# Branch products and sums moved to PSUM, and a first weight chunk with both tiles side by side

## The chip, the cores and the metric

The kernel runs on one core of one Trainium2 chip. The metric is the device time of one execution in microseconds (us). Five engines work side by side: TensorE (PE in the profile, its weight loads PEld), VectorE (DVE), ScalarE (ACT), GpSimd (POOL) and SyncE (SP, which issues transfers). On-chip memory is SBUF, and PSUM with eight banks of 128 x 512 float32; here four banks are called gemm0 to gemm3, four aux0 to aux3.

## The reference

Two transformer blocks on 256 tokens of width 1024, in float32. What is computed around the change, shortened:

```python
# first block
h = rmsnorm(x, norm1_g); z = h @ w_in            # first section of w_in: conv_in0..3
ya = conformer_conv(a_val, a_gate, ...)          # ... @ w_conv_out
yb = attention(...) @ w_fox_out
mix = (sigmoid(g_a) * ya + sigmoid(g_b) * yb) @ w_out       # kernel: mix_out
x = x + mix                                      # then expert layer, 64 chunks u and 64 ev
# second block
proj   = einsum("bsnc,ncd->bsnd", [out_a, out_b, out_c], w_branch)
merged = sum_n sigmoid(z_gate)[n] * proj[n]      # three gated branches
x = x + merged @ w_out                           # kernel: out2
# then the feed-forward layer and the final norm
```

## The kernel before, in words

Activations lie transposed, channels on partitions, as eight planes k of 128 x 256. Every weight matrix is cut into tiles of 128 x 1024, which give 128 output channels for all 256 tokens; two tiles (v = 0 and 1) make a chunk, whose two outputs fill one gemm bank. To keep float32 accuracy each factor is split into a rounded part ("hi") and the rest ("lo"), and a tile is 24 matmuls: eight hi x hi, eight with the activation's rest, eight with the weight's rest. The stages around a tile: SP loads `raw` (two buffers per v), ACT rounds it into `w_hi[v]` (L1285, in `round_tile`), POOL subtracts to get `w_lo[v]` (L460, in `subtract`), PE multiplies (L670 and L675 in `product_tile`; L691, L697, L716 and L722 in `paced_product`, which is used where the activation arrives in parts). There is one `w_hi` and one `w_lo` per v, so the rounding of the next tile v waits for `hi_used[v]`, and POOL's subtraction for the tile before it to be done. The order on each engine is the order of the code: ACT's `look_ahead` puts the weight roundings between its other work.

Three places matter.

- **The start.** PE runs 13 warming matmuls (L748), then the first chunk: tile 0 in `first_tile` (L734, L737, L742), tile 1 in `product_tile`. It works on x times gain, not yet normalised. ACT rounds x in four pairs of planes (L1323), rounds tile 1 and then squares x (L1328); DVE makes the rests (L1911) and adds the squares pair by pair (L1917, L1921, L1923); PE sums over partitions with a matrix of ones (L788); ACT takes the root (L1230), DVE the reciprocal (L1862) and the normalised planes (L1874), ACT rounds these (L1240), DVE forms h_lo (L1870). Chunk 1 (order[1]) still uses the unnormalised x; chunk 2 is the first with h, in `paced_product`.
- **fox_out to mix_out.** For each of the four chunks of fox_out, DVE multiplies the gate plane by the bank (L2076), adds the other branch (L2078), ACT rounds the sum (L1457), and DVE forms the rest (L2071, in `mix_rest`). mix_out opens with `paced_product`, whose parts wait for `y_rounded` and `y_split`.
- **branch2 and branch1 to out2.** `merge(b, i)` multiplies gate and bank (L2452) and adds to `merged` (L2456) for b = 2 and then b = 1; after b = 1 ACT rounds (L1750) and DVE forms the rest (L2461). Between the two lies the third gate's product, gate1. out2 opens with `paced_product` too. branch tiles are 128 x 768, 18 matmuls each.

`ga`, `gb`, `gate`, `merged` and `sq` are parts of one SBUF tensor, `big`, by which name they stand in the profile. Lines of the adds:

```python
dve.tensor_tensor(a, a, b, ALU.add).then_inc(mix_ready, 1)                     # L2078
dve.tensor_tensor(y_lo[:, part, :], ga[:, part, :], y_hi[:, part, :], ALU.subtract)   # L2071
```

Of the kernel before, what the change touches and what calls it, by code (L numbers as in the profile page):

```python
# [34 lines left out]
ALU = mybir.AluOpType  # L35
ACT = mybir.ActivationFunctionType
# [130 lines left out]
def build(nc, t):  # L167
    plan, order = plan_chunks()
    ctx = ExitStack()
    with ctx:  # L170
# [326 lines left out]
        def _(sp):  # L497
# [47 lines left out]
            sp.dma_start(params[:, GAIN1], t["params"][:, GAIN1]).then_inc(params_in, 16)  # L545
            load(order[0], 0, t["w_conv_in0"][0])
            for n in range(4):
                part = slice(2 * n, 2 * n + 2)
                sp.dma_start(xres[:, part, :], t["xT"].rearrange("(k p) t -> p k t", p=P)[:, part, :]).then_inc(x_in[n], 16)
            load(order[0], 1, t["w_conv_in0"][1])  # L550
            sp.dma_start(params[:, GAIN1.stop:], t["params"][:, GAIN1.stop:]).then_inc(params_in, 16)

            for name, chunks in plan.items():
# [3 lines left out]
                for i, c in enumerate(chunks):  # L557
                    for n, v in enumerate(c.landing):
                        if c.index == 0:
                            continue  # L560
                        if name in PACKED:
                            load_packed(name, c, v, 2 * i + v)
                        else:
                            load(c, v, t[f"w_{name}"][len(c.landing) * i + n])
                if name == "mem_k":
# [80 lines left out]
        def _(pe):  # L646
# [11 lines left out]
            def product_tile(c, v, m, it=None, x=(h_hi, h_lo), steps=KD, rest=None):  # L658
# [7 lines left out]
                for n, act_part in enumerate(x):  # L666
                    for k in range(steps):
# [58 lines left out]
            def first_tile(c, x, x_rest):  # L726

                out = pair(gemm[c.bank])[:, 0, :]
                hi, lo = by_k(w_hi[0], P), by_k(w_lo[0], P)
                pe.wait_ge(hi_ready[0], 1)  # L730
                for k in range(KD):
                    if k % 2 == 0:
                        pe.wait_ge(h_rounded, k // 2 + 1)
                    pe.matmul(out, hi[:, k, :], x[:, k, :], start=(k == 0), stop=False)  # L734
                    if k == 0:
                        pe.wait_ge(lo_ready[0], 1)
                    mm = pe.matmul(out, lo[:, k, :], x[:, k, :], start=False, stop=False)  # L737
                mm.then_inc(tile_done[0], 1)
                for k in range(KD):
                    if k % 2 == 0:  # L740
                        pe.wait_ge(h_split, k // 2 + 1)
                    mm = pe.matmul(out, hi[:, k, :], x_rest[:, k, :], start=False, stop=(k == KD - 1))  # L742
                mm.then_inc(hi_used[0], 1)

# [471 lines left out]
        def _(act):  # L1216
# [102 lines left out]
            act.wait_ge(params_in, 16)  # L1319
            for n in range(4):  # L1320
                act.wait_ge(x_in[n], 16)
# [3 lines left out]
            look_ahead(0)  # L1325
# [16 lines left out]
            act.wait_ge(params_in, 32)  # L1342
# [110 lines left out]
            for i in range(4):  # L1453
# [3 lines left out]
                act.activation(y_hi[:, part, :], ga[:, part, :], ACT.Copy).then_inc(y_rounded, 1)  # L1457
# [288 lines left out]
            for i in range(4):  # L1746
# [3 lines left out]
                act.activation(x_hi[:, part, :], merged[:, part, :], ACT.Copy).then_inc(m_rounded, 1)  # L1750
# [60 lines left out]
        def _(dve):  # L1811
# [95 lines left out]
            dve.wait_ge(params_in, 16)  # L1907
# [6 lines left out]
            subtract(dve, order[0], tiles=(1,))  # L1914
            running = aux[0][:, 0:T]
            dve.wait_ge(squared, 1)
            dve.tensor_tensor(running, sq[:, 0, :], sq[:, 1, :], ALU.add).then_inc(paired, 1)  # L1917
            for n in range(1, 4):
                dve.wait_ge(squared, n + 1)
                dve.wait_ge(paired, n)  # L1920
                step(dve.tensor_tensor(running, sq[:, 2 * n, :], running, ALU.add))  # L1921
                settle()
                dve.tensor_tensor(sq[:, 0, :] if n == 3 else running, sq[:, 2 * n + 1, :], running,  # L1923
# [22 lines left out]
            dve.wait_ge(params_in, 32)  # L1946
# [121 lines left out]
            def mix_rest(i):  # L2068
                part = slice(2 * i, 2 * i + 2)
                dve.wait_ge(y_rounded, 2 + i + 1)  # L2070
                dve.tensor_tensor(y_lo[:, part, :], ga[:, part, :], y_hi[:, part, :], ALU.subtract).then_inc(y_split, 1)  # L2071
# [372 lines left out]
            def merge(b, i):  # L2444
# [7 lines left out]
                dve.tensor_tensor(g, g, pair(gemm[c.bank]), ALU.mult).then_inc(evacuated[c.bank], 1)  # L2452
# [216 lines left out]
```

## Time and profile before

| | |
|---|---|
| median of 3 runs (lowest, highest) | 1609.11 us (1608.95, 1610.35) |
| profiled execution, its span | 1608.7 us, 1607.0 us |
| PE busy | 1587.3 us, 99% |
| DVE, POOL, ACT busy | 1101.3, 894.6, 882.2 us |
| DMA | 277.01 MB, mean 172 GB/s |

Busy times overlap, and a pipelined matmul is counted as busy from its start to its modelled end, so 99% does not mean that the matrix unit never waits; its waits are read from gaps between starts. Idle time of the other engines costs nothing unless PE waits for them.

### The profile page before, as it was taken

To read this page: it belongs to the slowest core of one execution; us is meant where nothing else is said; L and a number is where in the kernel's file an instruction comes from. 1 tells how busy PE (TensorE), PEld (TensorE's weight loads), DVE (VectorE), ACT (ScalarE), POOL (GpSimd) and SP (SyncE) were. 2 spreads that over 40 slices of the span, in tenths; PEclk is the share of its full clock that TensorE was granted. 3 is DMA by queue.
4 is the path that set the end of the run, shared out by engine and by line. 5 is a ranking of instruction groups with operands and counts; after the bars stand their busy time and mean duration, and the time that the engine had idled before them with its cause. 6 is when DMAs were issued, how large, how long until landed. Compare 5 with 4: busy or idle time off the path is not lost.

```text
span 1607.0 us, 33462 instructions
## 1 busy us (share of the span) xinstructions
PE 1587.3 (99%) x12561; PEld 1494.1 (93%) x12561; DVE 1101.3 (69%) x1869; ACT 882.2 (55%) x1241; POOL 894.6 (56%) x413
## 2 busy tenths in 40 slices
PE   9999999999999999999999999999999999999998
PEld 7999899999999999998888888889998999999998
DVE  7998645779943777778888666676847396555522
ACT  6567765454454444444444445457667654676652
POOL 7787468868885000000000244458876589788886
PEclk9999999999999999999999999999999999999999
DMA  6565345556566555555655666655543465566663
GB/s 216 166 194 156 105 132 178 189 174 191 184 183 189 165 180 170 171 158 183 179 162 183 211 191 195 192 183 165 179 138 111 115 179 173 175 194 185 191 186 119
DMA packets 86232, 277.01 MB, mean 172 GB/s; under 512 B 11248, under 2 KB 18176, under 8 KB 86144
## 3 DMA queue, kind: packets, MB, share of 16 engines
q1 hardware_dynamic: 85872, 274.77, 55.7%
q8 instruction: 58, 0.95, 0.3%
q0 software_dynamic: 272, 1.05, 0.2%
q14 instruction: 30, 0.25, 0.1%
HBM read 274.73 MB, written 1.05 MB: 172 GB/s over the span
## 4 chain that ended last, share of the span: by engine, by line
PE 92%; DVE 3%; issue 2%; POOL 2%; ACT 1%; DMA 0%; ACTq 0%; DVEq 0%; SPq 0%; POOLq 0%
PE gemm L670 36%; PE gemm L941 22%; PE gemm L675 19%; PE aux L1192 4%; PE gemm L771 3%; PE aux L921 2%; POOL w_lo L460 1%; PE gemm L716 1%; PE gemm L1192 1%; PE gemm L691 1%; PE aux L1047 0%; PE aux L891 0%; PE gemm L757 0%; DVE h_lo L1870 0%; ACT w_hi L1285 0%
## 5 line engine op out<-in xcount | busy, mean ns | idle before, releaser
L460 POOL TENSOR_TENSOR w_lo<-raw,w_hi 128x1024 fp32r<-128x1024 f32 (+1 forms) x330 | 797.6, 2426 | 298.3 <-ACT w_hi L1285 290.2
L1285 ACT ACTIVATE w_hi<-raw 128x1024 fp32r<-128x1024 f32 (+1 forms) x492 | 516.1, 1051 | 581.6 <-PE gemm L670 322.3
L670 PE MATMUL gemm<-h_lo,w_hi 128*128 128x256 f32 x2144 | 294.2, 279 | 0.9 <-issue 0.9
L670 PE MATMUL gemm<-h_hi,w_hi 128*128 128x256 f32 x2096 | 293.3, 282 | 0.4 <-ACT w_hi L1285 0.3
L675 PE MATMUL gemm<-h_hi,w_lo 128*128 128x256 f32 x2096 | 288.9, 280 | 1.4 <-POOL w_lo L460 0.9
L670 PEld LDWEIGHTS gemm<-h_lo,w_hi 128*128 128x128 f32 x2144 | 269.1, 188 | 1.4 <-issue 1.3
L460 DVE TENSOR_TENSOR w_lo<-raw,w_hi 128x1024 fp32r<-128x1024 f32 x162 | 196.7, 1223 | 105.2 <-ACT w_hi L1285 104.6
L670 PEld LDWEIGHTS gemm<-h_hi,w_hi 128*128 128x128 f32 x2096 | 264.2, 188 | 3.3 <-issue 1.6
L675 PEld LDWEIGHTS gemm<-h_hi,w_lo 128*128 128x128 f32 x2096 | 263.0, 188 | 3.9 <-POOL w_lo L460 2.8
L941 PE MATMUL gemm<-w_hi,act_parts 128*128 128x512 f32 x1024 | 254.9, 391 | 0.4 <-ACT act_parts L1486 0.4
L941 PEld LDWEIGHTS gemm<-w_hi,act_parts 128*128 128x128 f32 x1024 | 191.0, 188 | 39.6 <-issue 0.5
L616 POOL DMA_DIRECT2D small<-in_memT x1 | 1.0, 1029 | 383.6 <-DVE big L2216 383.6
L941 PE MATMUL gemm<-w_lo,act_parts 128*128 128x512 f32 x512 | 136.9, 389 | 0.0
L2222 DVE TENSOR_TENSOR act_parts<-big,act_parts 128x512 fp32r<-128x512 f32 x64 | 89.4, 1396 | 48.3 <-ACT act_parts L1486 48.3
L941 PEld LDWEIGHTS gemm<-w_lo,act_parts 128*128 128x128 f32 x512 | 96.0, 188 | 20.2 <-DVE w_lo L460 0.3
L1959 DVE SCALAR_TENSOR_TENSOR aux<-big,params,aux 128x256 f32<-128x256 f32 x240 | 94.7, 504 | 0.0
L456 POOL TENSOR_TENSOR w_lo<-raw,w_hi 128x768 fp32r<-128x768 f32 x30 | 61.0, 2035 | 17.6 <-ACT w_hi L1282 16.6
L2208 DVE TENSOR_TENSOR small<-small 128x512 f16<-128x512 f16 x128 | 57.2, 489 | 0.0
L2515 DVE SCALAR_TENSOR_TENSOR big<-gemm,params,big 128x255 f32<-128x255 f32 (+1 forms) x96 | 39.7, 476 | 25.0 <-ACT big L1763 25.0
L2205 DVE TENSOR_TENSOR small<-small 128x1024 f16<-128x1024 f16 x64 | 46.1, 720 | 0.0
L2216 DVE SCALAR_TENSOR_TENSOR big<-aux,big 128x512 f32 x64 | 41.1, 686 | 0.0
L1486 ACT ACTIVATE act_parts<-big 128x512 fp32r (+1 forms) x64 | 40.0, 627 | 0.2 <-issue 0.2
(425 smaller groups left out, 2085.1 us busy)
## 6 DMA issues: line engine op xcount, KB each, us to landing
raw<-in_w_u SPq DMA_DIRECT2D x128, 512.0 KB, 3.6
raw<-in_w_ev SPq DMA_DIRECT2D x128, 512.0 KB, 3.9
raw<-in_w_up SPq DMA_DIRECT2D x48, 512.0 KB, 4.3
raw<-in_w_gate SPq DMA_DIRECT2D x24, 512.0 KB, 3.6
raw<-in_w_down SPq DMA_DIRECT2D x24, 512.0 KB, 4.3
raw<-in_w_conv_in SPq DMA_DIRECT2D x16, 512.0 KB, 4.3
raw<-in_w_peer_q SPq DMA_DIRECT2D x16, 512.0 KB, 3.5
raw<-in_w_branch SPq DMA_DIRECT2D x24, 288.0 KB, 2.9
```

The source lines that it names most:

```text
L456: eng.tensor_tensor(lo[:, :, 0:C96], by_k(raw[c.raw][v], C96), hi[:, :, 0:C96], ALU.subtract)
L460: eng.tensor_tensor(w_lo[v][:, 0:n], raw[c.raw][v][:, 0:n], w_hi[v][:, 0:n], ALU.subtract).then_inc(lo_ready[v], 1)
L670: mm = pe.matmul(out, w[:, k, :], act_part[:, k, :], start=(n == k == 0), stop=False)
L675: mm = pe.matmul(out, w[:, k, :], x[0][:, k, :], start=False, stop=(k == steps - 1))
L771: mm = pe.matmul(pair(gemm[c.bank])[:, tt, :], x[:, v * KD // 2 + k, tt * P:(tt + 1) * P], w[:, k, :], start=(begins and tt == k == 0), st ...
L941: mm = pe.matmul(gemm[2 * half + tt][:, :], a[:, c.raw, v, tt * P:(tt + 1) * P], w[v][:, half * (D // 2):(half + 1) * (D // 2)], start=(op ...
L1192: mm = pe.matmul(out, w[v][:, k * P:(k + 1) * P], x[:, g * KD + k, :], start=(g == k == 0 and (v == 0 or pr == 3) and w is w_hi and x is f ...
L1285: act.activation(w_hi[v][:, 0:n], raw[c.raw][v][:, 0:n], ACT.Copy).then_inc(hi_ready[v], 1)
L1959: ins = dve.scalar_tensor_tensor(acc, zc[:, k, w:w + T], tap, acc, ALU.mult, ALU.add)
L2205: dve.tensor_tensor(hot2[:, b], each(iota2, P), along(e2T[:, tokens], P), ALU.is_equal)
L2208: ins = dve.tensor_tensor(hot1[:, b, part], hot[:, b], along(gate_parts[:, part, tokens], P // 2), ALU.mult)
L2222: dve.tensor_tensor(a_lo[:, c.raw, :, :], act_peer[:, plane, :], a_hi[:, c.raw, :, :], ALU.subtract).then_inc(a_split, 1)
```

## The change

(1) The gated products of fox_out, branch2 and branch1 go to an aux bank in PSUM, and so do the sums of fox_out and branch1; ACT rounds from there and DVE takes the rest from there. The sum of branch2 still goes to SBUF. (2) The first chunk interleaves its two tiles by pairs of planes as x arrives; SP loads tile 0, the first part of x, tile 1, then the other three parts; the first gains come by ACT's queue; the other parameters come behind chunk 1. ACT rounds tile 1 after the first pair of x, and DVE subtracts it after its first pair. (3) The squares are added in three steps of 128 x 512 in place of seven of 128 x 256, and the sum over partitions becomes two matmuls, placed inside chunk 1's first tile.

```diff
-            sp.dma_start(params[:, GAIN1], t["params"][:, GAIN1]).then_inc(params_in, 16)
-            load(order[0], 0, t["w_conv_in0"][0])
-            for n in range(4):
+            def load_x(n):
                 part = slice(2 * n, 2 * n + 2)
                 sp.dma_start(xres[:, part, :], ...).then_inc(x_in[n], 16)
+            load(order[0], 0, t["w_conv_in0"][0])
+            load_x(0)
             load(order[0], 1, t["w_conv_in0"][1])
-            sp.dma_start(params[:, GAIN1.stop:], t["params"][:, GAIN1.stop:]).then_inc(params_in, 16)
+            for n in range(1, 4):
+                load_x(n)
...
+                    if c.index == 1:
+                        sp.dma_start(params[:, GAIN1.stop:], ...).then_inc(params_in, 16)
...
+            def first_chunk(c, xh, xl):
...
+                for g in (1, 2):
+                    pe.wait_ge(h_rounded, g + 1)
+                    part(hi, 0, xh, g)
+                    part(lo, 0, xh, g)
+                    part(hi, 1, xh, g)
...
+                for g in (2, 3):
+                    pe.wait_ge(h_split, g + 1)
+                    mm = part(hi, 0, xl, g, ends=True)
                 mm.then_inc(hi_used[0], 1)
+                for g in (1, 2, 3):
+                    mm = part(hi, 1, xl, g)
+                mm.then_inc(hi_used[1], 1)
+                for g in (1, 2, 3):
+                    mm = part(lo, 1, xh, g, ends=True)
+                mm.then_inc(tile_done[1], 1)
+
+            def sum_first():
+                pe.wait_ge(paired, 4)
+                for k in range(2):
+                    mm = pe.matmul(aux[3][:, 0:T], ones[:, :], sq[:, k, :], start=(k == 0), stop=(k == 1))
+                mm.then_inc(sumsq, 1)
...
-            first_tile(order[0], *start_parts)
-            product_tile(order[0], 1, P, x=start_parts)
-            sum_gathered(0)
-            product(order[1], P, x=start_parts)
+            first_chunk(order[0], *start_parts)
+            product_tile(order[1], 0, P, x=start_parts, between=sum_first)
+            product_tile(order[1], 1, P, x=start_parts)
...
+            act.dma_start(params[:, GAIN1], t["params"][:, GAIN1]).then_inc(x_in[0], 16)
...
-                act.activation(y_hi[:, part, :], ga[:, part, :], ACT.Copy).then_inc(y_rounded, 1)
+                act.activation(y_hi[:, part, :], pair(aux[i]), ACT.Copy).then_inc(y_rounded, 1)
...
-                act.activation(x_hi[:, part, :], merged[:, part, :], ACT.Copy).then_inc(m_rounded, 1)
+                act.activation(x_hi[:, part, :], pair(aux[i]), ACT.Copy).then_inc(m_rounded, 1)
...
+            running = pair(aux[0])
+            dve.wait_ge(squared, 2)
+            dve.tensor_tensor(running, sq[:, 0:2, :], sq[:, 2:4, :], ALU.add).then_inc(paired, 2)
...
-                dve.tensor_tensor(b, b, pair(gemm[c.bank]), ALU.mult).then_inc(evacuated[c.bank], 1)
+                dve.tensor_tensor(pair(aux[i]), b, pair(gemm[c.bank]), ALU.mult).then_inc(evacuated[c.bank], 1)
                 moved(dve, [c, plan["conv_out"][i]])
-                dve.tensor_tensor(a, a, b, ALU.add).then_inc(mix_ready, 1)
+                dve.tensor_tensor(pair(aux[i]), a, pair(aux[i]), ALU.add).then_inc(mix_ready, 1)
...
-                dve.tensor_tensor(g, g, pair(gemm[c.bank]), ALU.mult).then_inc(evacuated[c.bank], 1)
+                gated = pair(aux[i])
+                dve.tensor_tensor(gated, g, pair(gemm[c.bank]), ALU.mult).then_inc(evacuated[c.bank], 1)
...
-                dve.tensor_tensor(m, m, g, ALU.add).then_inc(merge_done, 1)
+                dve.tensor_tensor(gated if b == 1 else m, m, gated, ALU.add).then_inc(merge_done, 1)
...
-                dve.tensor_tensor(m_lo[:, part, :], merged[:, part, :], x_hi[:, part, :], ALU.subtract).then_inc(m_split, 1)
+                dve.tensor_tensor(m_lo[:, part, :], pair(aux[i]), x_hi[:, part, :], ALU.subtract).then_inc(m_split, 1)
```

PE's order at the start, before, from the first tile to the sum over partitions (gemm0 is the first chunk's bank; w_hi0 and w_hi1 are its tiles 0 and 1; x_hi and x_lo are x times gain, rounded and rest):

```order
L737 MATMUL gemm0<-x_hi,w_lo0 128x256
L742 MATMUL gemm0<-x_lo,w_hi0 128x256 x8
L670 MATMUL gemm0<-x_hi,w_hi1 128x256 x8
L670 MATMUL gemm0<-x_lo,w_hi1 128x256 x8
L675 MATMUL gemm0<-x_hi,w_lo1 128x256 x8
L788 MATMUL aux3<-big,ones 128x256
L670 MATMUL gemm1<-x_hi,w_hi0 128x256 x8
```

PE's order there now, from the third pair of planes on:

```order
L740 MATMUL gemm0<-x_hi,w_lo1 128x256 x2
L740 MATMUL gemm0<-x_lo,w_hi0 128x256 x2
L740 MATMUL gemm0<-x_hi,w_hi0 128x256 x2
L740 MATMUL gemm0<-x_hi,w_lo0 128x256 x2
L740 MATMUL gemm0<-x_hi,w_hi1 128x256 x2
L740 MATMUL gemm0<-x_lo,w_hi0 128x256 x4
L740 MATMUL gemm0<-x_lo,w_hi1 128x256 x6
L740 MATMUL gemm0<-x_hi,w_lo1 128x256 x6
L677 MATMUL gemm1<-x_hi,w_hi0 128x256 x8
L782 MATMUL aux3<-big,ones 128x256 x2
```

Tile 0's last use of w_hi0 now stands 12 matmuls ahead of the chunk's end, where 24 stood behind it; the sum has moved behind eight matmuls of chunk 1.

DVE's order in branch1 before, the last two of the four chunks (big is gate and merged in SBUF):

```order
L2452 TENSOR_TENSOR big<-big,gemm1 128x512
L2456 TENSOR_TENSOR big<-big 128x512
L2461 TENSOR_TENSOR m_lo<-big,x_hi 128x512
L2452 TENSOR_TENSOR big<-big,gemm2 128x512
L2456 TENSOR_TENSOR big<-big 128x512
L2461 TENSOR_TENSOR m_lo<-big,x_hi 128x512 x2
```

and now:

```order
L2490 TENSOR_TENSOR aux2<-big,gemm1 128x512
L2494 TENSOR_TENSOR aux2<-big,aux2 128x512
L2499 TENSOR_TENSOR m_lo<-aux1,x_hi 128x512
L2490 TENSOR_TENSOR aux3<-big,gemm2 128x512
L2494 TENSOR_TENSOR aux3<-big,aux3 128x512
L2499 TENSOR_TENSOR m_lo<-aux2,x_hi 128x512
L2499 TENSOR_TENSOR m_lo<-aux3,x_hi 128x512
```

Nothing has moved there; every instruction that read two SBUF operands now reads one, the other coming from an aux bank.

## Rows read from the trace of the kernel before

**Rows 1.** Page: TensorE's granted clock in 40 slices, tenths of full speed.
```profile
PEclk9999999999999999999999999999999999999999
```
**Rows 2.** DVE instructions by line: count, ns min/median/max, start us first to last.
```profile
L2078 DVE TENSOR_TENSOR big<-big x4: 753/828/1962, 236.7 to 254.3; 128x512 f32<-128x512 f32 x4
L2071 DVE TENSOR_TENSOR y_lo<-big,y_hi x4: 677/2886/2894, 243.7 to 257.8; 128x512 fp32r<-128x512 f32 x4
L2456 DVE TENSOR_TENSOR big<-big x8: 1024/1778/2191, 1325.4 to 1369.6; 128x512 f32<-128x512 f32 x8
L2503 DVE TENSOR_TENSOR gemm<-gemm,rstd x24: 690/700/700, 1402.8 to 1529.8; 128x512 f32<-128x512 f32 x24
```
**Rows 3.** Timeline of the start: start us, duration us, engine, line, [idle before <-releaser].
```profile
1.74 1.96 SPq L549 DMA_DIRECT2D xres<-in_xT  x4
...
5.50 1.06 ACT L1285 ACTIVATE w_hi<-raw 128x1024 fp32r<-128x1024 f32 x1 [3.18 <-DMA raw<-in_w_conv_in]
10.00 1.07 ACT L1285 ACTIVATE w_hi<-raw 128x1024 fp32r<-128x1024 f32 x1 [0.24 <-DMA raw<-in_w_conv_in]
...
10.98 2.18 ACT L1328 ACTIVATE big<-xres 128x512 f32<-128x512 f32 x4
...
15.74 0.70 PE L788 MATMUL aux<-big,ones 128*128 128x256 f32 x2 [1.12 <-DVE big L1923]
...
21.27 1.07 ACT L1285 ACTIVATE w_hi<-raw 128x1024 fp32r<-128x1024 f32 x1
...
21.96 1.91 PE L691 MATMUL gemm<-h_hi,w_hi 128*128 128x256 f32 x12
22.24 1.13 ACT L1240 ACTIVATE h_hi<-big 128x512 fp32r<-128x512 f32 x2
```
**Rows 4.** Transfers issued from 3.4 to 3.8 us: KB each, us from issue to landing.
```profile
raw<-in_w_conv_in SPq DMA_DIRECT2D x1, 512.0 KB, 6.2
xres<-in_xT SPq DMA_DIRECT2D x1, 256.0 KB, 5.4
```
**Rows 5.** Chain of waits around fox_out and mix_out: start us, duration us, engine, line.
```profile
235.69 2.42 POOL w_lo L460
...
250.72 1.89 PE gemm L670 x16
...
253.60 0.70 DVE big L2076
...
254.32 0.75 DVE big L2078
255.07 3.42 DVE y_lo L2071 x2
...
258.54 1.45 PE gemm L716 x10
```
**Rows 6.** Timeline of POOL around branch1, columns as in rows 3.
```profile
1355.31 1.85 POOL L460 TENSOR_TENSOR w_lo<-raw,w_hi 128x768 fp32r<-128x768 f32 x1 [0.29 <-ACT w_hi L1285]
1359.18 14.25 POOL L460 TENSOR_TENSOR w_lo<-raw,w_hi 128x768 fp32r<-128x768 f32 x6 [2.02 <-ACT w_hi L1285]
```
**Rows 7.** Chain of waits from gate1 to out2, columns as in rows 5.
```profile
1343.94 1.21 PE gemm L675 x8
...
1355.00 1.42 PE gemm L670 x12
...
1369.62 1.56 DVE big L2456
1371.18 3.41 DVE m_lo L2461 x2
...
1374.63 1.45 PE gemm L716 x10
```
**Rows 8.** POOL by form, 1323.4 to 1350.5 us: count, busy us, mean ns.
```profile
L460 POOL TENSOR_TENSOR w_lo<-raw,w_hi 128x1024 fp32r<-128x1024 f32 x8 | 22.2, 2808 | 0.0
L460 POOL TENSOR_TENSOR w_lo<-raw,w_hi 128x768 fp32r<-128x768 f32 x2 | 4.9, 2439 | 0.3 <-ACT w_hi L1285 0.3
```

More of the change, by code:

```diff
@@ L656, in bank_free, with product_tile @@
                     pe.wait_ge(evacuated[c.bank], c.bank_use - 1)
-            def product_tile(c, v, m, it=None, x=(h_hi, h_lo), steps=KD, rest=None):
+            def product_tile(c, v, m, it=None, x=(h_hi, h_lo), steps=KD, rest=None, between=None):
                 if v == 0:
@@ L666, in product_tile @@
                 for n, act_part in enumerate(x):
+                    if n and between:
+                        between()
                     for k in range(steps):
@@ L724, in paced_product, with part @@
                 mm.then_inc(tile_done[1], 1)
-            def first_tile(c, x, x_rest):
-                out = pair(gemm[c.bank])[:, 0, :]
-                hi, lo = by_k(w_hi[0], P), by_k(w_lo[0], P)
-                pe.wait_ge(hi_ready[0], 1)
[L731 to L742, printed above, removed]
-                mm.then_inc(hi_used[0], 1)
+            def first_chunk(c, xh, xl):
+                both = pair(gemm[c.bank])
+                hi, lo = [by_k(w, P) for w in w_hi], [by_k(w, P) for w in w_lo]
+                def part(w, v, x, g, begins=False, ends=False):
+                    for k in (2 * g, 2 * g + 1):
+                        mm = pe.matmul(both[:, v, :], w[v][:, k, :], x[:, k, :], start=(begins and k == 0),
+                                       stop=(ends and k == KD - 1), skip_group_check=True)
+                    return mm
+                pe.wait_ge(hi_ready[0], 1)
+                pe.wait_ge(h_rounded, 1)
+                part(hi, 0, xh, 0, begins=True)
+                pe.wait_ge(lo_ready[0], 1)
+                part(lo, 0, xh, 0)
+                pe.wait_ge(hi_ready[1], 1)
+                part(hi, 1, xh, 0)
+                pe.wait_ge(h_split, 1)
+                part(hi, 0, xl, 0)
+                part(hi, 1, xl, 0)
+                for g in (1, 2):
[3 more added lines that the diff above has]
+                    part(hi, 1, xh, g)
+                pe.wait_ge(lo_ready[1], 1)
+                part(lo, 1, xh, 0)
+                pe.wait_ge(h_split, 2)
+                part(hi, 0, xl, 1)
+                pe.wait_ge(h_rounded, 4)
+                part(hi, 0, xh, 3)
+                part(lo, 0, xh, 3).then_inc(tile_done[0], 1)
+                part(hi, 1, xh, 3)
+                for g in (2, 3):
+                    pe.wait_ge(h_split, g + 1)
+                    mm = part(hi, 0, xl, g, ends=True)
+                mm.then_inc(hi_used[0], 1)
+                for g in (1, 2, 3):
[4 more added lines that the diff above has]
+                mm.then_inc(tile_done[1], 1)
@@ L1318, in _ @@
             look_ahead(0, 1)
-            act.wait_ge(params_in, 16)
             for n in range(4):
-                act.wait_ge(x_in[n], 16)
+                act.wait_ge(x_in[n], 32 if n == 0 else 16)
                 for k in (2 * n, 2 * n + 1):
@@ L1324, in _ @@
                 ins.then_inc(h_rounded, 1)
-            look_ahead(0)
+                look_ahead(0)
             for n in range(4):
@@ L1913, in _ @@
                 ins.then_inc(h_split, 1)
[L1914 to L1918, printed above, removed]
+                if n == 0:
+                    subtract(dve, order[0], tiles=(1,))
+            running = pair(aux[0])
+            dve.wait_ge(squared, 2)
+            dve.tensor_tensor(running, sq[:, 0:2, :], sq[:, 2:4, :], ALU.add).then_inc(paired, 2)
+            for n in (2, 3):
                 dve.wait_ge(squared, n + 1)
                 dve.wait_ge(paired, n)
-                step(dve.tensor_tensor(running, sq[:, 2 * n, :], running, ALU.add))
-                settle()
-                dve.tensor_tensor(sq[:, 0, :] if n == 3 else running, sq[:, 2 * n + 1, :], running,
+                dve.tensor_tensor(sq[:, 0:2, :] if n == 3 else running, sq[:, 2 * n:2 * n + 2, :], running,
                                   ALU.add).then_inc(paired, 1)
@@ L1945, in _ @@
             gated_values(0)
-            dve.wait_ge(params_in, 32)
+            dve.wait_ge(params_in, 16)
             for j in range(4):
@@ L2070, in mix_rest @@
                 dve.wait_ge(y_rounded, 2 + i + 1)
-                dve.tensor_tensor(y_lo[:, part, :], ga[:, part, :], y_hi[:, part, :], ALU.subtract).then_inc(y_split, 1)
+                dve.tensor_tensor(y_lo[:, part, :], pair(aux[i]), y_hi[:, part, :], ALU.subtract).then_inc(y_split, 1)
             for i, c in enumerate(plan["fox_out"]):
```

4 lines of the change are left out of this document (2 added, 2 removed).

## The prediction, made before the changed kernel ran

> **What bounds the kernel now.** I read the page first: PE is busy 99% of the span, and the granted clock is full in each of the 40 slices [rows 1]. So the time is the number of matmuls times their distance, 1.89 us for 16 or 0.118 us each [rows 5], plus the gaps in which PE waits. The change adds only two passes (below), so it can only win or lose in the gaps. The table of waits and then the chain of waits show where they are. Three places belong to this change: the start [rows 3], the passage from fox_out to mix_out [rows 5], and the stretch from branch2 over gate1 and branch1 to out2 [rows 6 to 8]. The reader should see in the chains that PE's own lines give way there to DVE and POOL.
>
> The reason for the last two is in the durations by line. DVE's additions and subtractions of 128x512 with both operands in SBUF take 0.68 to 0.75 us at best and up to 2.89 us [rows 2]. The long ones lie where POOL subtracts weights, also from SBUF. An undisturbed POOL tile takes 2.42 us at 1024 columns [rows 5] and 1.85 at 768 [rows 6]; a DVE subtraction of 2.89 is some 0.7 of work after 2.2 of waiting for one such tile. POOL pays too: ten tiles that should take 8 x 2.42 + 2 x 1.85 = 23.1 us took 22.2 + 4.9 = 27.1 [rows 8], and six that should take 4 x 1.85 + 2 x 2.42 = 12.2 took 14.25 [rows 6].
>
> The nearest row for what comes instead is the feed-forward scaling, which reads one operand from PSUM and writes PSUM: 24 times 0.690 to 0.700 us, with POOL at work beside it [rows 2]. Twenty instructions change in this way: 12 sums and 8 rests. I take 0.69 for each. The bounds: 0.69, and the median of the same line now, if the operand in PSUM frees nothing.
>
> The Trainium skill (SBUF — State Buffer, Who interferes with whom) says that a VectorE instruction with two SBUF inputs contends with a GpSimd instruction that reads SBUF, and one with at most one such input does not. These rows agree on the lengths. The same skill (VectorE: DVE Perf Modes, the section on the TRN2 errata) speaks against the change: it charges 120 cycles of overhead for a PSUM source and 58 for an SBUF source, some 0.065 us more. As an estimate from that page, the sum and two rests that close each of two passages would lose 0.4 us together; the scaling's 0.700 against 0.68 to 0.75 doesn't show it, and no term rests on it.
>
> **The start.** SP's first issue, the gains, moves to ACT's queue, so every transfer of SP starts some 0.44 us earlier (my estimate: SP issues x's four parts in 1.96 us, 0.49 each, and this one is small). Today the last part of x lands about 5.4 us after its issue near 1.74 + 3 x 0.49 = 3.2, at 8.6, and tile 1 at 10.0 [rows 3, 4]. Afterwards tile 1 lands near 7.1, and the last part of x, now last of the same bytes, near 9.6. ACT then rounds it until 10.7, squares (2.18 us) until 12.9, and rounds chunk 1's first tile until 13.9; today the squares end at 13.16 [rows 3], so ACT, nearly without a gap from 5.50 on in either order, gives only 0.3 us. PE: DVE has the last rest of x ready near 12.3, 14 matmuls (1.65 us) are left, chunk 0 ends near 13.9. So chunk 1 starts at 13.9, where it starts near 16.1 today behind the sum's first half and its 1.12 us of waiting for DVE's seven additions [rows 3]. These become three of 0.7 us and are done at 14.5, before PE asks for them at 14.9. The sum has four passes in place of two (0.22 us each more, estimated; at most 0.35 by the 0.70 for two) and is there near 15.95, not 16.44.
>
> PE would thus reach chunk 2 near 20.5, and not at 21.96, but chunk 2 needs h. The whole chain of root, reciprocal, normalised planes and roundings hangs on the sum and moves by 0.5; the rounding of chunk 2's tile 1, which stands between h's second and third part on ACT, moves from 21.27 to about 20.6, and the last two parts with it [rows 3]. So what is late next is h on ACT, and of the 1.4 us PE keeps 0.6. Bounds: a loss of 1.0, if x's parts land a whole 512 KB later and the 0.44 is not had, and a gain of 1.4, if h is no limit. I take 0.6, as the chain is made of ACT and DVE rows with known lengths.
>
> The other parameters, now behind chunk 1, are needed only by the convolution, over ten us later: nothing. DVE's subtraction of tile 1 stands before six of its rests and is covered by the earlier landing; without that cover the rests, chunk 0 and chunk 1 would be late by as much as it takes.
>
> **fox_out to mix_out.** After the last fox_out matmul, the chain is product 0.70, sum 0.75, then two rests of 3.42 us together, and the last ten matmuls of mix_out's rest part begin at 258.54 [rows 5]. Fox_out's last matmuls end at 250.72 + 24 x 0.118 = 253.57; the opening has 24 matmuls with the rounded parts, so without a wait its 16 rest matmuls would begin at 256.4 and the last ten at 257.1. With 0.69 each the rests are ready by 256.5. The gain is 258.54 - 257.1 = 1.4 us. Bounds: 0, and 1.9, if PE also waited half a microsecond less for the POOL tile that stands on the chain at 235.69. I take 1.4: DVE would have to be over 0.6 us late to touch it.
>
> **branch2 and gate1.** Four sums here go from 1.8 to 2.2 us down to 0.69. POOL is busy without a break, and PE waits for it in places: eight matmuls took 1.21 us at 1343.94 for 0.94 [rows 7, 8], and there are two like it and a smaller one, 0.88 in all. Of POOL's 4.0 lost us I give 4 x 0.7 to the four sums; the rest belongs to three longer instructions that stay. That is enough to end the unbroken run, so I take 0.8 of the 0.88. Bounds 0 and 0.9.
>
> **branch1 to out2.** From 1355.00 to the end of the rest matmuls in out2's opening, 148 matmuls at 0.118 should take 17.5 us. They take 21.1: the last ten rest matmuls begin at 1374.63 and need 1.45 [rows 7]. The 3.6 us of gaps are one chain: a sum of 1.8 us (the median) makes ACT round late, so POOL starts at 1359.18 after 2.02 us idle [rows 6], then is stretched to 14.25 us, then sum and two rests of 1.56 and 3.41 us stand on the path [rows 7]. With 0.69 each, ACT rounds 1.1 us sooner, POOL needs 12.2 us, and the rests are ready before PE asks. Left is some 0.3 for the rounding of out2's second tile. I take 3.3; bounds 1.8 (the tail alone, POOL as now) and 3.6.
>
> **Sum.** 0.6 + 1.4 + 0.8 + 3.3 = 6.1 us. From the profiled execution's own 1608.7 us that is 1602.6. The median of the runs is 0.4 above that execution, so I forecast 1603.0. A later stage should keep the gain: whatever comes after is released by PE or through it.
>
> **The rivals.**
>
> *POOL is not relieved.* DVE's changed instructions get short, but POOL keeps its stretched lengths, for the other SBUF operands or for another reason. For it: POOL's loss isn't shown instruction by instruction. Against it: the lost 4.0 and 2.1 us lie just where DVE reads twice from SBUF. Then branch2 gives 0 and branch1 1.8: 0.6 + 1.4 + 1.8 = 3.8, so 1605.3.
>
> *The operand in PSUM frees nothing.* The long DVE times come from something else that stays. Only the start is left: 1608.5, no change. The 24 short rows beside a busy POOL speak against it.
>
> *The start gives nothing back.* x lands later behind tile 1, and h comes as now: 5.5 us, so 1603.6; with the loss of 1.0 it is 1604.6. For it: three quarters of x now queue behind 512 KB.
>
> *Slower: the clock.* Today the granted clock is full everywhere [rows 1], the first matmuls come 1.4 us behind the warming ones, and the first tile is sparse. Now PE's work between 7 and 12.3 us is 34 matmuls, 4.0 us, in more and smaller pieces. If the clock fell to 1.2 GHz, each matmul would cost 0.118 more. It decides from 52 slow matmuls on, just over one chunk; with the first two chunks slow, 96, it costs 11.3 us: 1614.3. The Trainium skill (TensorE: Matmul & The Clock Gate) describes such a fall after low activity; here no row shows a fall, and today's first tile has gaps as well.
>
> **How the numbers follow.** Forecast 0.55 (1602 to 1604, all terms as above); POOL not relieved 0.18; start gives nothing 0.10; PSUM frees nothing 0.08; slower by the clock 0.04; 0.05 for more than 6.1, as all upper bounds together give 1.4 + 1.9 + 0.9 + 3.6 = 7.8, or 1601.3. What a measurement of this kernel can tell from no change is 0.2%, 3.2 us: faster is below 1605.9. Faster gets 0.55 + 0.10 + 0.05 and most of the first rival, 0.83 in all; the same gets 0.13; slower 0.04. The range runs from 1601.2 to 1606.2 and leaves out the two cases that give no gain and a little on either side.
>
> **What would show it.** In the changed profile every changed DVE line reads 0.68 to 0.70 us, minimum and maximum alike. The waits of mix_out and out2 for DVE's rests are gone. POOL's six tiles in branch1 take about 12.2 us, and its run through gate1 has gaps. At the start, PE's sum stands near 15 us, and chunk 2 begins with a short wait for ACT. I am wrong if changed lines still exceed 1 us, if PE waits in their place for POOL or for w_hi, or if the granted clock dips in the first 20 us.

## The result, and the profile after the change

The changed kernel takes 1603.54 us (median of 7 runs, 1602.51 to 1604.58), against 1609.03 us for the kernel before in 7 runs on the same chip (1608.35 to 1610.35): 0.9963 of the time, 95% interval 0.9954 to 0.9972, so 5.5 us less, with an interval that stays clear of 1. The forecast was 1603.0. Its profiled execution took 1602.92 us, with a span of 1601.2 where it was 1607.0. A later series on another chip gave 1602.58 us beside 1609.47, ratio 0.9960 (0.9947 to 0.9974).

The page first, with its busy times. Its granted clock reads 9 in each of the 40 slices, as in [rows 1]; a 9 stands for 90% or more, so it can hide a short fall in a slice of 40 us, and in both kernels it hides one at the end of the span (below). VectorE (DVE) lost 26 us of busy time (1101.3 before), GpSimd (POOL) 6, TensorE (PE) 2.

```profile
PE 1585.3 (99%) x12563; PEld 1494.5 (93%) x12563; DVE 1075.1 (67%) x1865; ACT 880.7 (55%) x1241; POOL 888.4 (55%) x413
```

The rows that answer to [rows 2], rests and sums by line (ns min/median/max, start us first to last). L2108 was L2071, L2115 was L2078, L2499 was L2461, L2494 was L2456:

```profile
L2108 DVE TENSOR_TENSOR y_lo<-aux,y_hi x4: 682/683/691, 242.3 to 254.4; 128x512 fp32r<-128x512 f32 x4
L2115 DVE TENSOR_TENSOR aux<-big,aux x4: 695/696/697, 235.4 to 253.1; 128x512 f32<-128x512 f32 x4
L2499 DVE TENSOR_TENSOR m_lo<-aux,x_hi x4: 683/683/692, 1357.6 to 1366.9; 128x512 fp32r<-128x512 f32 x4
L2494 DVE TENSOR_TENSOR big<-big,aux x4: 686/686/687, 1323.2 to 1327.2; 128x512 f32<-128x512 f32 x4
L2494 DVE TENSOR_TENSOR aux<-big,aux x4: 695/696/696, 1352.8 to 1365.5; 128x512 f32<-128x512 f32 x4
```

Minimum and maximum are 10 ns apart or less, where they were up to 2217 ns apart. The chain of waits around the passage to mix_out, answering to [rows 5]: start us, duration us, engine, line.

```profile
252.29 1.59 PE gemm L698 x12
...
255.42 1.89 PE gemm L723 x16
```

There is no DVE piece left in it. All 16 rest matmuls (L723, before L716) run at 0.118 us. The same chain at out2, answering to [rows 7]:

```profile
1364.14 1.07 ACT w_hi L1324
...
1365.25 1.33 PE gemm L698 x9
...
1368.00 1.89 PE gemm L723 x16
```

Here one ACT piece remains, the rounding of out2's second tile. POOL in the same stretch (timeline of POOL, columns as in [rows 6]) and through gate1 (by form, count, busy us and mean ns as in [rows 8]):

```profile
1354.89 3.66 POOL L460 TENSOR_TENSOR w_lo<-raw,w_hi 128x768 fp32r<-128x768 f32 x2 [0.75 <-ACT w_hi L1324]
1359.15 3.65 POOL L460 TENSOR_TENSOR w_lo<-raw,w_hi 128x768 fp32r<-128x768 f32 x2 [0.60 <-ACT w_hi L1324]
1363.63 4.75 POOL L460 TENSOR_TENSOR w_lo<-raw,w_hi 128x1024 fp32r<-128x1024 f32 x2 [0.83 <-ACT w_hi L1324]
```

```profile
L460 POOL TENSOR_TENSOR w_lo<-raw,w_hi 128x1024 fp32r<-128x1024 f32 x8 | 20.1, 2539 | 0.5 <-ACT w_hi L1324 0.3
```

Four tiles of 768 and two of 1024 take 3.66 + 3.65 + 4.75 = 12.06 us, where they took 14.25, and eight tiles through gate1 take 2.54 us in the mean, where they took 2.81.

The start, timeline of ACT, columns as in [rows 3]:

```profile
6.79 1.06 ACT L1324 ACTIVATE w_hi<-raw 128x1024 fp32r<-128x1024 f32 x1 [0.19 <-DMA raw<-in_w_conv_in]
7.75 2.50 ACT L1362 ACTIVATE x_hi<-xres,params 128x256 fp32r<-128x256 f32 x6
10.16 2.18 ACT L1367 ACTIVATE big<-xres 128x512 f32<-128x512 f32 x4
12.31 2.01 ACT L1324 ACTIVATE w_hi<-raw 128x1024 fp32r<-128x1024 f32 x2
15.55 0.48 ACT L1269 ACTIVATE std<-aux,epsc 128x256 f32<-128x256 f32 x1 [1.22 <-PE aux L782]
...
20.08 1.04 ACT L1324 ACTIVATE w_hi<-raw 128x1024 fp32r<-128x1024 f32 x1
```

To see where time comes and goes I compare, in the traces of two kernels, the start of the same group of matmuls, counted from the start of each span. The table gives the shift against the one profile of before; what matters is the difference between two columns.

| kernel | at 46.8 us | mix_out's 13th matmul, 254.98 | after its opening, 259.8 | before branch2, 1250 | after gate1, 1355 | after out2's opening, 1375.9 | end |
|---|---|---|---|---|---|---|---|
| changed | -1.20 | -1.26 | -2.67 | -2.19 | -3.01 | -6.19 | -5.78 |
| e12, the same again | -1.05 | -1.10 | -2.51 | -2.59 | -3.46 | -6.62 | -6.68 |
| e1, products and sums alone | -0.10 | 0.38 | -1.03 | 0.19 | -0.63 | -3.80 | -3.83 |
| e2, start alone | -0.99 | -1.03 | -1.03 | -0.87 | -0.80 | -0.81 | -0.83 |
| e3, sums in SBUF | -1.01 | -1.05 | -2.14 | -2.23 | -3.10 | -5.12 | -3.62 |
| e4, products in SBUF | -0.85 | -0.40 | -1.35 | -1.28 | -1.25 | -1.73 | -1.46 |
| e8, branch2 in SBUF | -0.33 | -0.37 | -1.77 | -1.90 | -1.89 | -5.05 | -4.55 |
| e10, two SBUF inputs more | -0.64 | -0.70 | -2.11 | -1.25 | -1.24 | -4.38 | -4.42 |
| e11, one SBUF input more | 1.11 | 1.04 | -0.37 | 0.24 | -0.64 | -3.80 | -3.33 |

So the changed kernel won 1.2 us at the start, 1.4 at mix_out, 0.8 at gate1 and 3.2 from branch1 to out2, 6.6 in all. It ended with 5.8: it gave back 0.2 us at 337 us, 0.4 between 437 and 507 us and 0.4 in its last four matmuls, and small shifts the other way leave 0.8. Its twin e12 gave back nothing in sum. The second column stands 12 matmuls into mix_out's opening. In e4 PE has already waited there, so its gain at this passage is the difference between the first column and the third, 0.5 us.

The loss in the last four matmuls (L1249, L1210 in the kernel before) is the clock's. They took 0.73 us at full clock before and in e12, and 1.17 in the changed kernel's profile, first as a piece of the chain, then as a window of PE (stretch, its length, PE busy (matmuls), granted clock, DMA share, GB/s):

```profile
1594.15 1.17 PE gemm L1249 x4
```

```profile
1594.00:1595.00 1.00, 0.85 (x4) 0.63 0.00 0
```

Every profile shows the clock at 0.50 at the end of the span; what differs is whether it falls before or behind the last of these four. In the changed kernel, e3, e4, e5, e8 and e11 it fell before, and the four took 1.01 to 1.24 us; in the other eight profiles they took 0.72 or 0.73.

### The profile page after: what moved, and what is told of

It is laid out like the page before. It is cut to its first block, busy times and chain, and to the rows that moved or that the text cites. A ratio compares the mean times of both kernels' runs of the same rounds, so it can differ in the third digit from the quotient of the medians.

```text
span 1601.2 us, 33460 instructions
## 1 busy us (share of the span) xinstructions
PE 1585.3 (99%) x12563; PEld 1494.5 (93%) x12563; DVE 1075.1 (67%) x1865; ACT 880.7 (55%) x1241; POOL 888.4 (55%) x413
## 3 DMA queue, kind: packets, MB, share of 16 engines
q0 software_dynamic: 272, 1.05, 0.2%
HBM read 274.73 MB, written 1.05 MB: 172 GB/s over the span
## 4 chain that ended last, share of the span: by engine, by line
PE 92%; DVE 2%; issue 2%; POOL 2%; ACT 1%; DMA 1%; SPq 0%; ACTq 0%; DVEq 0%; POOLq 0%
PE gemm L677 36%; PE gemm L980 22%; PE gemm L682 18%; PE aux L1231 4%; PE gemm L811 3%; PE aux L960 2%; POOL w_lo L460 1%; PE gemm L698 1%; PE gemm L723 1%; PE gemm L1231 1%; ACT w_hi L1324 0%; PE aux L1086 0%; PE aux L930 0%; PE gemm L797 0%; DVE h_lo L1909 0%
```

## The experiments

Theory: a DVE instruction with two SBUF inputs and a POOL instruction on SBUF can't run at once; an operand in PSUM takes DVE out of this, so both get their own lengths, and PE waits for neither. The main rival: DVE's changed lines get short, but POOL isn't relieved. A second one is that what counts is where the result is written, and not what is read; e3 and e4 tell the two apart.

**e1 and e2, each half alone, 5 rounds.** e1 is the kernel before with the diff's lines on products, sums, roundings and rests; e2 the changed kernel with these lines undone, as in

```diff
-                dve.tensor_tensor(pair(aux[i]), a, pair(aux[i]), ALU.add).then_inc(mix_ready, 1)
+                dve.tensor_tensor(a, a, b, ALU.add).then_inc(mix_ready, 1)
```

> The kernel before with the PSUM edits alone (products and sums of fox_out and branch1, products of branch2 in the aux banks). Theory (the port is freed, each passage gains by itself): 5.4 to 5.6 us of the chain go at the three passages (1.4, 0.9, 3.2), so about 1604.4 us; start as before, first matmul of the fourth chunk at 28.1. Rival (the two parts need each other): under 3 us of gain.

> The changed kernel with the PSUM edits undone; the start is the changed one. Theory: the fourth chunk starts at 27.0 us and not at 28.1, the passages are as before, so 1608.0 us (0.9 to 1.2 less than before). Rival (the start's gain is given back at a later wait that doesn't move with it): 1609.0 us, no change, while the fourth chunk starts at 27.0.

e1 took 1604.39 us, ratio 0.9968 (0.9956 to 0.9980); e2 1608.55, ratio 0.9995 (0.9986 to 1.0004), both beside 1609.50 for before. The products and sums carry 5 of the 5.5 us. The start alone is below what five rounds can tell; its trace has it at 0.8 to 1.0. The halves don't disturb each other: mix_out, gate1 and out2 give 1.41, 0.82 and 3.17 us in e1 and nothing in e2.

**e3 and e4, sums or products alone back in SBUF.** In e3 the product stays in PSUM and the sum goes to SBUF, so each rest reads twice from SBUF. In e4 the product goes to SBUF, so each sum reads twice from SBUF, and only the sum lies in PSUM.

```diff
# e3
-                dve.tensor_tensor(pair(aux[i]), a, pair(aux[i]), ALU.add).then_inc(mix_ready, 1)
+                dve.tensor_tensor(a, a, pair(aux[i]), ALU.add).then_inc(mix_ready, 1)
...
# e4
-                dve.tensor_tensor(pair(aux[i]), b, pair(gemm[c.bank]), ALU.mult).then_inc(evacuated[c.bank], 1)
+                dve.tensor_tensor(b, b, pair(gemm[c.bank]), ALU.mult).then_inc(evacuated[c.bank], 1)
...
-                dve.tensor_tensor(pair(aux[i]), a, pair(aux[i]), ALU.add).then_inc(mix_ready, 1)
+                dve.tensor_tensor(pair(aux[i]), a, b, ALU.add).then_inc(mix_ready, 1)
...
```

> The changed kernel with the sums of fox_out and branch1 written to SBUF again (products still in PSUM), so that ACT and the rests read SBUF. Theory (a DVE instruction contends with POOL when both its inputs are in SBUF): sums stay at 0.69 us, as they read one SBUF operand; the eight rests go back to a median over 2.3 us; PE waits about 0.9 us for the last rests at mix_out and again at out2; 1 to 2.5 us slower than the changed kernel. Rival (writing to SBUF is what costs): the sums too go back over 1 us.

> The changed kernel with the gated products written to SBUF again, the sums of fox_out and branch1 in PSUM. Now the sums read two SBUF operands and the rests one. Theory: the 12 sums go back to 1 to 2.2 us, the rests stay at 0.69; of the 1.32 us of the fox_out passage some 0.9 stay, gate1's 0.85 are lost, and in branch1 to out2 some 1.2 to 1.5 of the 3.3 stay. Rival (any 128x512 operation gets short once its result is in PSUM): the sums of fox_out and branch1 at 0.7.

e3: 1604.84 us, ratio 0.9968 (0.9957 to 0.9979), which time alone can't tell from the changed kernel's 0.9963. e4: 1607.24 us in one run beside 1609.62. The sums of fox_out and branch1 show that the inputs decide. With one SBUF input and the result in SBUF they are short (e3); with two SBUF inputs and the result in PSUM they are long (e4):

```profile
L2494 DVE TENSOR_TENSOR big<-big,aux x8: 686/686/687, 1323.1 to 1365.4; 128x512 f32<-128x512 f32 x8
```

```profile
L2494 DVE TENSOR_TENSOR aux<-big x4: 1529/2160/2720, 1354.5 to 1368.1; 128x512 f32<-128x512 f32 x4
```

In e3 the last two rests of out2 are on the chain again, in 3.35 us for two, and cost 1.2 of the 3.2 us there; at mix_out 0.3 of 1.4.

```profile
1366.13 3.35 DVE m_lo L2499 x2
1369.48 0.04 issue
1369.52 1.44 PE gemm L723 x10
```

e4 is the larger loss, and I had its size wrong: of 1.4 and 3.2 us it keeps only 0.5 and 0.5. The chain shows the last sum of each passage blocked behind a POOL tile, ahead of ACT's rounding, so the rounded part itself comes late and PE waits within the opening:

```profile
253.43 1.66 DVE aux L2115
255.09 0.02 issue
255.11 0.61 ACT y_hi L1496
...
1368.08 2.73 DVE aux L2494
```

A blocked sum costs more than a blocked rest. Behind the last sum stand ACT's rounding, the last six of the opening's 24 matmuls with rounded parts, and the rest; a blocked rest holds up only its own part of the 16 rest matmuls, and PE has the 24 to do meanwhile. A blocked sum also holds up what ACT does next. In e4 ACT sat idle for 3.09 us before its rounding at 1366.23, and only then rounded out2's two tiles; PE waited 0.60 and 0.27 us for these, 0.19 for POOL's `w_lo` and 0.21 for the last rounded part.

**e8, e10 and e11, what relieves POOL at gate1.** e8 undoes branch2's product only. e10 and e11 leave the change as it is and add one DVE instruction ahead of each of branch2's four sums; its output is read by nobody. It reads twice from SBUF in e10, once in e11.

```diff
# e8
-                gated = pair(aux[i])
+                gated = pair(aux[i]) if b == 1 else g
# e10
+                if b == 2:
+                    dve.tensor_tensor(g, g, m, ALU.add)
# e11
+                if b == 2:
+                    dve.tensor_tensor(g, g, gated, ALU.add)
```

> branch2's gated product goes to SBUF again, all else as changed. If the 0.8 us at gate1 come from branch2's sums leaving the shared port to GpSimd, they are gone, and only they: PE 0.8 us later than in the changed kernel from 1344 us on, VectorE's four sums back at 2.04 us and GpSimd's tiles at 2.81, and the 3.3 us of branch1 and out2 kept: 1604.2 to 1604.5 us. Rival: that branch2's products matter for the chain at out2 too, since GpSimd falls behind there: then 1604.9 us or more.

> One more VectorE instruction ahead of each of branch2's four sums, over 128x512, that reads gate and merged, both in SBUF, and writes gate, which nothing reads after it. Theory of the port: it is held, or holds GpSimd, as the old sums were (2.04 us each and GpSimd's tiles at 2.81 us in the mean): VectorE's new instructions take 0.7 to 2.7 us each, GpSimd's 128x1024 tiles between 1323 and 1350 us rise from 2.54 to 2.7 to 2.85 us in the mean, PE waits for w_lo again at gate1 and the 0.8 us won there are gone: 1604.2 to 1604.6 us. Rival, that the gain came from VectorE's time alone: the same loss here and in the twin that reads one operand from PSUM.

> The twin: the same four extra instructions, but the second operand is the product in PSUM. Theory of the port: 0.69 us each, no effect on GpSimd (its 128x1024 tiles stay at 2.54 us), no wait at gate1, 1603.3 to 1603.9 us. Rival, that VectorE's time alone decides: it loses as much as its twin, 0.8 us.

One run each: e8 1604.15 us, e10 1604.28, e11 1605.37. The time of e11 is no measure of this step, since it lost 1.4 us at its start (below). The step itself is read from POOL by form from 1323 to 1350.5 us and from DVE's added instruction, first e10, then e11:

```profile
L460 POOL TENSOR_TENSOR w_lo<-raw,w_hi 128x1024 fp32r<-128x1024 f32 x8 | 22.2, 2808 | 0.0
...
L2493 DVE TENSOR_TENSOR big<-big 128x512 f32<-128x512 f32 x4 | 6.4, 1589 | 0.1
```

```profile
L460 POOL TENSOR_TENSOR w_lo<-raw,w_hi 128x1024 fp32r<-128x1024 f32 x8 | 20.1, 2529 | 0.5 <-ACT w_hi L1324 0.3
...
L2493 DVE TENSOR_TENSOR big<-big,aux 128x512 f32<-128x512 f32 x4 | 2.7, 686 | 0.1
```

Four instructions of the same size on the same engine: with two SBUF inputs POOL's tiles are back at 2.81 us, as before the change and as in e8 (2.807), and the 0.8 us at gate1 are gone in both (0.0 in the table). With one, POOL keeps 2.53 and gate1 keeps 0.88 us. Four more DVE instructions, 2.7 us of work, cost gate1 nothing in e11; the second SBUF input does. e8 and e10 keep the 3.2 us at branch1, so the two places are independent.

**e5 and e6, the transfers of the start.** e5 issues the gains first on SP again. e6 loads all of x before tile 1 again.

```diff
# e5
+            sp.dma_start(params[:, GAIN1], t["params"][:, GAIN1]).then_inc(x_in[0], 16)
             load(order[0], 0, t["w_conv_in0"][0])
...
-            act.dma_start(params[:, GAIN1], t["params"][:, GAIN1]).then_inc(x_in[0], 16)
# e6
-            load_x(0)
-            load(order[0], 1, t["w_conv_in0"][1])
-            for n in range(1, 4):
+            for n in range(4):
                 load_x(n)
+            load(order[0], 1, t["w_conv_in0"][1])
```

> The changed kernel with the gains issued first on SP's queue, as before. Theory (one issue less ahead of the weights): everything of the start is 0.44 us later, so ACT rounds the first tile at 5.2 and not 4.74 us, and the fourth chunk starts 0.4 to 0.5 us later than in the changed kernel. Rival (the gains' 128 small packets also hold up the weights on the same queue): 0.7 us later or more. Rival 2 (the start is bound elsewhere): the fourth chunk starts within 0.1 us of the changed kernel.

> The changed kernel with all of x ahead of tile 1 in SP's queue. ACT's order is unchanged, so it waits for tile 1 after the first pair of x. Theory: tile 1 lands near 9.3 us and not 6.8, ACT idles 2.5 us and everything behind it moves: the fourth chunk starts 2.0 to 2.5 us later than in the changed kernel, and later than in the kernel before. Rival (order of these two transfers hardly matters, bandwidth does): under 1 us later.

One run each: e5 1604.40 us, e6 1607.19. In e5 the roundings of tiles 0 and 1 begin at 5.46 and 8.25 us, 0.7 and 1.5 later than in the changed kernel, and the shift at 46.8 us is +0.32, 1.5 later. I had expected 0.4 to 0.5; as landings alone vary by up to 1.2 us between profiles, one profile can't say how much of the rest is the queue's. In e6 it is +3.33, 4.5 later. Tile 1's rounding begins at 8.90, which explains 2.1. The rest was in the granted clock. Windows of PE in e6, columns as in the window above:

```profile
8.00:9.00 1.00, 0.00 (x0) 0.94 1.05 422
9.00:10.00 1.00, 0.00 (x0) 0.50 1.02 410
10.00:11.00 1.00, 0.99 (x4) 0.50 0.99 388
...
14.00:15.00 1.00, 1.00 (x7) 0.50 0.19 78
15.00:16.00 1.00, 1.00 (x8) 0.65 0.00 0
```

PE, waiting for tile 1, had no work from 8 to 10 us (2.44 us idle in all); the clock fell to its lower level, 1.2 GHz, and stayed there for over 6 us. Between 10 and 16 us that loses up to 5 x 0.50 + 0.35 = 2.85 us of matmul work. So the new order of the matmuls needs the new order of tile 1 and x: the clock rival exists, and it shows around the gap before tile 1. e11, whose start is the changed kernel's, shows the same from 9 us on:

```profile
8.00:9.00 1.00, 0.05 (x1) 1.00 1.07 396
9.00:10.00 1.00, 1.00 (x5) 0.57 1.03 408
10.00:11.00 1.00, 1.00 (x7) 0.50 1.02 403
11.00:12.00 1.00, 1.00 (x7) 0.50 1.05 394
12.00:13.00 1.00, 1.00 (x8) 0.73 1.00 394
```

It lost up to 0.43 + 0.50 + 0.50 + 0.27 = 1.7 us of work; its shift is 1.44 above that of e8, whose tile 1 came at nearly the same time (rounded from 7.75 us, e11 from 7.84) and whose clock stayed full:

```profile
8.00:9.00 1.00, 0.15 (x1) 1.00 1.06 396
9.00:10.00 1.00, 1.00 (x9) 1.00 1.02 414
```

Nor is the length of the gap what decides. e9 (below) waited longer for tile 1 than e11, and its clock stayed full:

```profile
8.97 0.50 PE L740 MATMUL gemm<-x_hi,w_hi 128*128 128x256 f32 x2 [1.37 <-ACT w_hi L1324]
```

So the changed start can lose its clock behind a late tile 1, but need not. Of ten profiles whose first 13 us are the changed kernel's (e7 and e9 below among them), one did, e11. The Trainium skill (TensorE: Matmul & The Clock Gate, What's actually happening) says that the point at which the clock changes varies from run to run, since it isn't counted from the kernel's start; e8, e11 and e9, idle for 1.19, 1.20 and 1.37 us before tile 1, with a fall in e11 alone, agree with that.

**e7 and e9, two attempts at a better start, both misses.** e7 computes the sum over partitions ahead of chunk 1 and not inside it. e9 (5 rounds) rounds tile 1 of chunk 2 after the second pair of normalised planes and not after the third, since PE waits 0.56 us for it.

```diff
# e7
+            sum_first()
-            product_tile(order[1], 0, P, x=start_parts, between=sum_first)
+            product_tile(order[1], 0, P, x=start_parts)
# e9
-            round_h(0, beside=lambda q: look_ahead(2) if q == 2 else None)
+            round_h(0, beside=lambda q: look_ahead(2) if q == 1 else None)
```

> The changed kernel with the sum over partitions ahead of chunk 1, not inside it. Theory: DVE's three additions end near 13.9, PE waits 0.3 us for them and the sum is there 0.6 us sooner (14.9 and not 15.5), and as chunk 2 waits for h and not for PE, the fourth chunk starts 0.1 to 0.5 us sooner than in the changed kernel. Rival (PE is what is late): 0.3 us later.

> ScalarE rounds tile 1 of chunk 2 after its second pair of normalised tiles and not after the third, about 0.7 us earlier. In the changed kernel PE waits 0.56 us for it at 21.18 us, in the chain. If the chain there is what it shows, the wait shrinks and the product from there on is 0.3 to 0.5 us earlier: 1603.1 to 1603.3 us against 1603.5, a ratio of 0.9997 to 0.9998 to the changed kernel, at the edge of what the rounds can tell; the landmarks of the trace tell it better, beside a start that varies by 0.3. If instead ScalarE's rounded pairs are needed as early as the tile (paced product), the wait only changes its name (to h_hi) and nothing is won, or 0.1 to 0.3 is lost.

e7: 1605.38 us in one run. e9: 1605.35 us, ratio to before 0.9971 (0.9960 to 0.9982) where e12 on the same chip has 0.9960 (0.9947 to 0.9974); the intervals overlap, and the traces decide. Tile 1 landed later in both (rounded from 7.73 and 7.86), but e8 at 7.75 stands at -0.33 from 46.8 us on, and these at +1.29 and +1.73. The four h_lo rests of chunk 2 (ns min/median/max), first in e7, then in e9, and last the POOL tile that runs beside these rests in the changed kernel:

```profile
L1910 DVE TENSOR_TENSOR h_lo<-big,h_hi x4: 675/682/2881, 21.3 to 25.3; 128x512 fp32r<-128x512 f32 x4
```

```profile
L1909 DVE TENSOR_TENSOR h_lo<-big,h_hi x4: 677/678/2476, 22.0 to 25.6; 128x512 fp32r<-128x512 f32 x4
```

```profile
21.20 4.55 POOL L460 TENSOR_TENSOR w_lo<-raw,w_hi 128x1024 fp32r<-128x1024 f32 x1 [0.63 <-ACT w_hi L1324]
```

In the changed kernel DVE starts its four rests at 20.99 us, without a gap, before POOL's tile at 21.20: DVE keeps 0.69 us each and POOL's tile takes 4.55 us in place of 2.41, which nobody waits for. In e7 and e9 POOL is in its tile when a rest comes, and that rest takes 2.9 and 2.5 us. Behind it DVE's next work, then ACT's roundings for chunk 3 (at 27.61 and 27.88, 25.11 in the changed kernel) and PE are late. It is one lock with either side as loser, and on DVE it costs more. In e9, moving one ACT instruction of 1 us decided who came first. The Trainium skill (SBUF — State Buffer, Who interferes with whom) says just this: "Issue order, not op shape, decides who blocks." The rows agree.

**e12, the changed kernel once more, 5 rounds.**

> The changed kernel itself, once more and on this chip. It measures how far two profiled runs of one program stand apart at the start (transfers) and by the stretches in which matmuls are 0.118 us apart and not 0.117. If the start of the first profile (1.2 us earlier than before at 27.9 us) was partly luck, this one shows 0.6 to 1.0 there; if it is the program's, 1.1 to 1.3. The time: 1603.0 to 1604.2 us.

1602.58 us. Its start is 1.05 earlier, its three later gains 1.41, 0.87 and 3.16. It doesn't give back 0.4 us between 437 and 507 us, nor 0.4 in the last four matmuls, as the first profile does.

## Why the prediction was right

**The mechanism and its prices.** Predicted: every changed DVE line at 0.68 to 0.70 us. They read 0.682 to 0.697. The bounds were fair, and the near row, a line that reads and writes PSUM beside a busy POOL [rows 2], was the right one to take. The rival that the operand in PSUM frees nothing falls with e1, and e3 and e4 show that it is the inputs that decide.

**fox_out to mix_out, 1.4.** Measured 1.40 or 1.41 in six profiles and 0.0 in e2. The step was made right: fox_out's last matmul, then 40 matmuls at 0.118 without a stop.

**branch2 and gate1, 0.8.** Measured 0.82 to 0.88 in five profiles, 0.0 in e8 and e10. The share of POOL's loss given to the sums was checked too: from 2.81 to 2.54 us for eight tiles is 2.1 us, where 2.8 had been taken. It sufficed, as PE needed 0.88.

**branch1 to out2, 3.3.** Measured 3.14 to 3.18 in six profiles. What stays is the rounding of out2's second tile, as said. The rival in which POOL is not relieved is false: its six tiles take 12.06 us (12.2 predicted). e10 and e11 are the proof that it is the second SBUF input that slows it.

**The start, 0.6: the term with the wrong size.** Measured 1.2 in the first profile; in the eight profiles with that start the shift at 46.8 us is -1.20, -1.05, -1.01, -0.99, -0.85, -0.64, -0.33 and +1.11, median -0.92. Part of it is the baseline: e1, with the old start code, is itself 0.27 early at 23.7 us, as its first tile was rounded from 4.82 us and not 5.50. Against e1 the median is 0.65, seven lie between 0.1 and 0.9, and one is a loss of 1.4. What failed is the step on landings: "tile 1 lands near 7.1, and the last part of x near 9.6". Tile 1 was there at 6.7 or 6.8 in two profiles, near 7.0 in three and 7.4 to 7.8 in three others, and x's last rounding ended at 10.25, not 10.7. From there each step came some 0.5 us earlier than written: squares done at 12.3 (12.9), chunk 1 at 13.5 (13.9), the sum at 15.5 (15.95), chunk 2's tile 1 at 20.08 (20.6). The order of events was as predicted, with h on ACT as what is late next and a wait of 0.56 us in chunk 2.

**The clock, 4 in 100.** In the changed kernel's profile it didn't happen at the start. As a mechanism it is real, and its place was named, but its size was not: 1.4 us in e11, not 11.3. The clock was back after 3.4 us (some 7 in e6), and in no run did the fall last for two chunks; and at the lower level matmuls stand 0.215 us apart (four in 0.86 us from 11.12 us on in e11), so each costs 0.10 more and not 0.118. As the trigger the prediction named sparse work in the first chunk; both falls came at the gap in which PE waits for tile 1, and what decides between e11 and e9 stays open. The prediction also read the nines of [rows 1] as a clock full everywhere. The windows of that trace show it full over the start and the middle, but at 0.50 behind the last matmuls, from 1602.6 us on; in the changed kernel's profile this fall came early enough to cost 0.4 us.

**The sum.** 6.1 predicted; 6.6 won by place, and 5.8 left in the span, 6.7 in e12. That the total came so near is partly luck: the start gave 0.6 more than its term, and 0.8 was given back, for which the prediction had no term. The give-back has three parts. Some 0.4 us is the clock under the last four matmuls. About 0.2 went with a transfer that came late: PE waited for the tile behind it at 336 us. Another 0.4 lies in a stretch in which nothing was changed and matmuls at a granted clock of 1.00 stand 0.118 us apart and not 0.117, which makes 0.15 us in 16 us. Such stretches sit elsewhere in each profile (e1 from 48 to 98 and 355 to 507 us, e3 from 1425 to 1530). Their cause is open; I have no experiment on it.

## What to carry to other kernels

Look at minimum, median and maximum of one line's instructions: a line of equal shapes that spans 0.7 to 2.9 us is not slow, it is blocked, and the value to expect once it is free is the shortest that an instruction of this kind and size takes anywhere in the trace, here 0.68 to 0.70. A line's own minimum can be a blocked one: the sums of L2456 had 1024 ns at best [rows 2] and came down to 686. Where DVE reads two SBUF operands beside a busy POOL, put one of them in a free PSUM bank, first for the instruction on which the most queued work depends. Reordering the first transfers and reordering the first matmuls belong together: the new matmuls with the old transfers opened a gap at which the clock fell (e6); the old matmuls with the new transfers were not run. And a page with nines in all slices can hide a fallen clock of some us: ask for narrow windows at the start and at the end.

## What the runs showed of the hardware

- The block is mutual: one h_lo of 2881 ns against its 682, or one POOL tile of 4.55 us against 2.41. In the second case POOL stood behind all four rests, which follow each other without a gap (20.99 + 2.49 = 23.48, and 2.41 more make 25.89; the tile ended at 25.75): it did not get in between two of them.
- Operands in PSUM cost next to nothing: 0.686 us for a sum written to SBUF and 0.696 for one written to PSUM; a rest from PSUM took 0.683, an unblocked one from SBUF 0.682. Where a sum is written decides nothing: with one SBUF input and the result in SBUF it took 0.686 (e3), with two SBUF inputs and the result in PSUM 1.53 to 2.72 (e4, branch1). The Trainium skill (VectorE: DVE Perf Modes, the section on the TRN2 errata) charges 62 cycles more for a PSUM source; these rows don't show them.
- The granted clock fell to 0.50 behind a sparse stretch with a gap of 1.20 us (e11), and not with one of 1.19 (e8) or of 1.37 (e9). It stayed down 3.4 us in e11 and over 6 in e6, where PE had no work for 2 us. It fell again at the end of every profile; where that came before the last matmul, the last four took 1.01 to 1.24 us (six profiles), and 0.72 or 0.73 elsewhere (eight).
- The same transfers land up to 1.2 us apart between executions: tile 1's rounding, with the start unchanged, began between 6.69 and 7.86 us.
